# A 64-token chunk of a delta-rule recurrence on one core: three tiles of the block inverse move to the other half of the partitions, and one transpose moves behind the first level

## The reference, cut to what matters

```python
def step(S, inp):
    r_t, w_t, k_t, v_t, kk_t, a_t = inp
    sa = jnp.einsum('bhvk,bhk->bhv', S, -kk_t)
    S = (S * w_t[:, :, None, :] + sa[..., None] * (kk_t * a_t)[:, :, None, :]
         + v_t[..., None] * k_t[:, :, None, :])
    return S, jnp.einsum('bhvk,bhk->bhv', S, r_t)
```

## Time and profile before

| | us |
|---|---|
| median of 3 runs | 2737.84 |
| the three runs | 2737.84, 2742.84, 2735.46 |
| the profiled execution, its own time | 2741.77 |
| span of the profiled execution | 2740.1 |
| PE busy (share of the span) | 2511.4 (92%) |
| PE weight loads busy | 2473.5 (90%) |
| DVE busy | 1479.8 (54%) |
| ACT busy | 967.4 (35%) |
| granted clock of PE, mean | 0.935 |

### The profile page before, as it was taken

One profiled execution on the slowest core, in us unless ns is written; L12 is line 12 of the kernel. 1 busy time (PEld: TensorE's weight loads), 2 busy tenths in 40 slices (PEclk: granted clock), 3 DMA queues, 4 the chain that ended last, 5 costly groups with the idle time before them and its releaser, 6 DMA issues.

```text
span 2740.1 us, 57636 instructions
## 1 busy us (share of the span) xinstructions
PE 2511.4 (92%) x22966; PEld 2473.5 (90%) x22966; DVE 1479.8 (54%) x1889; ACT 967.4 (35%) x1159; POOL 97.5 (4%) x162
## 2 busy tenths in 40 slices
PE   8999999999999979988967546689999999999999
PEld 8999999999989978988967445589999999999999
DVE  6555555555666674544434462157565545554554
ACT  5333333333454432222202112054443333333333
POOL 0000000000110000000000000001200000000000
PEclk9999999999999989999956775589999999999999
DMA  6665665555545533333411410155555555555555
GB/s 232 209 229 184 205 218 181 182 181 184 165 164 194 174 120 123 110 101 101 134 65 33 142 67 28 52 190 188 185 183 179 182 179 182 184 180 181 182 167 174
DMA packets 120235, 432.49 MB, mean 158 GB/s; under 512 B 14232, under 2 KB 16408, under 8 KB 119328
## 3 DMA queue, kind: packets, MB, share of 16 engines
q1 hardware_dynamic: 112896, 393.49, 43.3%
q0 software_dynamic: 7200, 36.93, 3.9%
HBM read 417.34 MB, written 23.50 MB: 161 GB/s over the span
## 4 chain that ended last, share of the span: by engine, by line
PE 87%; DVE 4%; DMA 3%; DVEq 2%; ACT 2%; issue 1%; POOL 0%; ACTq 0%; SPq 0%; POOLq 0%
PE bank L249 25%; PE bank L250 25%; PE bank L251 25%; PE bank L1061 5%; DMA side<-stg 1%; PE bank L1154 1%; PE bank L1156 1%; PE bank L1163 1%; DVE qn L950 1%; PE bank L1252 1%; PE bank L1283 1%; DMA gates<-side 1%; DVE wlo L223 1%; DVE gn L915 0%; DVE nrm L812 0%
## 5 line engine op out<-in xcount | busy, mean ns | idle before, releaser
L223 DVE TENSOR_TENSOR wlo<-raw,whi 128x1024 fp32r<-128x1024 f32 (+2 forms) x762 | 907.0, 1197 | 688.5 <-ACT whi L217 680.3
L249 PE MATMUL bank<-hhi,whi 128*128 128x264 f32 x4048 | 1161.6, 287 | 24.0 <-DVE hlo L284 12.3
L250 PE MATMUL bank<-hlo,whi 128*128 128x264 f32 x4048 | 1150.7, 284 | 0.0
L251 PE MATMUL bank<-hhi,wlo 128*128 128x264 f32 x4048 | 1149.6, 284 | 0.0
L217 ACT ACTIVATE whi<-raw 128x1024 fp32r<-128x1024 f32 (+2 forms) x762 | 786.1, 1034 | 1021.9 <-PE bank L251 1017.8
L249 PEld LDWEIGHTS bank<-hhi,whi 128*128 128x128 f32 x4048 | 766.3, 189 | 31.2 <-DVE wlo L223 12.5
L250 PEld LDWEIGHTS bank<-hlo,whi 128*128 128x128 f32 x4048 | 767.1, 190 | 0.3
L251 PEld LDWEIGHTS bank<-hhi,wlo 128*128 128x128 f32 x4048 | 762.7, 188 | 0.0
L249 PE MATMUL bank<-mhi,whi 128*128 128x264 f32 x1408 | 399.6, 284 | 0.0
L250 PE MATMUL bank<-mlo,whi 128*128 128x264 f32 x1408 | 399.1, 283 | 0.0
L251 PE MATMUL bank<-mhi,wlo 128*128 128x264 f32 x1408 | 399.0, 283 | 0.0
(11 more groups left out here) (279 smaller groups left out, 1989.3 us busy)
## 6 DMA issues: line engine op xcount, KB each, us to landing
raw<-in_weights SPq DMA_DIRECT2D x666, 512.0 KB, 3.3
raw<-in_weights SPq DMA_DIRECT2D x64, 384.0 KB, 3.1
raw<-in_weights SPq DMA_DIRECT2D x32, 448.0 KB, 3.8
out_skv<-in_cache POOLq DMA_DIRECT2D x16, 512.0 KB, 3.8
side<-stg POOLq DMA_DIRECT2D x50, 132.0 KB, 3.3
gates<-side POOLq DMA_DIRECT2D x1, 4224.0 KB, 16.0
qkv<-side POOLq DMA_DIRECT2D x1, 2376.0 KB, 10.2
x<-in_x SPq DMA_DIRECT2D x4, 528.0 KB, 6.7
```

The costliest lines, as they stand in the source:

```text
L223: dve.tensor_tensor(wlo[:, s, 0:n], raw[:, s, 0:n], whi[:, s, 0:n].bitcast(F32), ALU.subtract).then_inc(lo_done, 1)
L249: pe.matmul(bank[:, 0:T], hi, xhi[:, k], start=(k == 0), stop=False)
L250: pe.matmul(bank[:, 0:T], hi, xlo[:, k], start=False, stop=False)
L251: mm = pe.matmul(bank[:, 0:T], lo, xhi[:, k], start=False, stop=(k == kt - 1))
```

## The change

`per_head` gets two arguments: `frm=1` takes the operands of head p from the other half of the partitions, and `to=1` puts the result there. `qm`, `m1` and `w1` of a head now lie in the other half. `qm` can therefore no longer be cut from `ab`. It is made from a second product `bc`·`ar` of its own (bank 3), beside `ar`·`bc` (bank 2), which is moved up from the groups behind extra(0). The wide `kc`/`ar` product takes its place behind extra(0), in banks 0 and 1. `per_head_twice` issues two groups interleaved, pair by pair: the two `ar`/`bc` products, and in levels 1 to 4 the two additions `m1`·`qm` and `qm`·`m1`. With these halves the two products of a pair and a side use all four quarters of the array. The transpose of `kc` moves behind the second groups of level 1, with a semaphore `c_kt`, and ACT's copy to `kt_` moves behind the copy of `m1` of level 1 and waits for it.

```diff
@@ -665,13 +665,16 @@
                 act.activation(pi[:], cum[:, :, cols], ACT.Exp, scale=DECAY).then_inc(c_exp, 1)
                 act.activation(vc[:], V_[:, :, cols], ACT.Copy).then_inc(c_op, 1)
                 extra(0)
-                act.wait_ge(c_pe, 9 * c + 3)
-                for dst, bank in ((vt, 1), (bt, 2), (kt_, 3)):
+                act.wait_ge(c_pe, 10 * c + 4)
+                for dst, bank in ((vt, 2), (bt, 3)):
                     act.activation(dst[:], A4[bank][:].rearrange("p (j n) -> p j n", n=C), ACT.Copy).then_inc(c_act, 1)
                 extra(1)
                 for lv in range(1, 6):
                     act.wait_ge(c_m1, 5 * c + lv)
                     act.activation(m1[:], A4[0][:].rearrange("p (j n) -> p j n", n=C), ACT.Copy).then_inc(c_act, 1)
+                    if lv == 1:
+                        act.wait_ge(c_kt, c + 1)
+                        act.activation(kt_[:], A4[3][:].rearrange("p (j n) -> p j n", n=C), ACT.Copy).then_inc(c_act, 1)
                     extra(1 + lv)
                 act.wait_ge(c_w1, 2 * c + 1)
                 act.activation(w1[:], A4[3][:].rearrange("p (j n) -> p j n", n=C), ACT.Copy).then_inc(c_act, 1)
@@ -839,25 +842,24 @@
                 dve.tensor_copy(pend[:], pc[:, :, C - 1])
                 dve.drain()
                 dve.sem_inc(c_vec, 1)
-                dve.wait_ge(c_pe, 9 * c + 1)
+                dve.wait_ge(c_pe, 10 * c + 1)
                 for q in range(2):
                     dve.tensor_tensor(ab[:, 4 * q:4 * q + 4], A4[q][:].rearrange("p (j n) -> p j n", n=2 * C),
                                       over(cc("causal"), 4), ALU.mult)
                 dve.drain()
                 dve.sem_inc(c_vec, 1)
-                dve.wait_ge(c_pe, 9 * c + 2)
-                for q in range(2):
-                    dve.tensor_tensor(ak[:, 4 * q:4 * q + 4], A4[2 + q][:].rearrange("p (j n) -> p j n", n=2 * C),
-                                      over(cc("causal"), 4), ALU.mult)
+                dve.wait_ge(c_pe, 10 * c + 2)
+                dve.tensor_tensor(tm[:], A4[2][:].rearrange("p (j n) -> p j n", n=C), over(cc("join0t"), PAIRS), ALU.mult)
+                dve.tensor_tensor(qm[:], A4[3][:].rearrange("p (j n) -> p j n", n=C), over(cc("join0"), PAIRS), ALU.mult)
                 dve.drain()
                 dve.sem_inc(c_vec, 1)
-                dve.tensor_tensor(qm[:], ab[:, :, 0:C], over(cc("join0"), PAIRS), ALU.mult)
-                extra(0)
-                dve.wait_ge(c_pe, 9 * c + 3)
-                dve.tensor_tensor(tm[:], A4[0][:].rearrange("p (j n) -> p j n", n=C), over(cc("join0t"), PAIRS), ALU.mult)
-                dve.drain()
                 dve.tensor_tensor(qm[:], qm[:], over(cc("ident64"), PAIRS), ALU.add)
                 dve.tensor_tensor(tm[:], tm[:], over(cc("ident64"), PAIRS), ALU.add)
+                extra(0)
+                dve.wait_ge(c_pe, 10 * c + 3)
+                for q in range(2):
+                    dve.tensor_tensor(ak[:, 4 * q:4 * q + 4], A4[q][:].rearrange("p (j n) -> p j n", n=2 * C),
+                                      over(cc("causal"), 4), ALU.mult)
                 for lv in range(1, 6):
                     dve.tensor_tensor(zm[:], ab[:, :, 0:C], over(cc(f"join{lv}"), PAIRS), ALU.mult)
                     dve.drain()
@@ -865,14 +867,14 @@
                     if lv == 1:
                         extra(1)
                     extra(1 + lv)
-                    dve.wait_ge(c_pe, 9 * c + 3 + lv)
+                    dve.wait_ge(c_pe, 10 * c + 4 + lv)
                     dve.tensor_tensor(qm[:], qm[:], A4[1][:].rearrange("p (j n) -> p j n", n=C), ALU.add)
                     if lv < 5:
                         dve.tensor_tensor(tm[:], tm[:], A4[2][:].rearrange("p (j n) -> p j n", n=C), ALU.add)
                 dve.drain()
                 dve.sem_inc(c_lv, 1)
                 extra(7)
-                dve.wait_ge(c_pe, 9 * c + 9)
+                dve.wait_ge(c_pe, 10 * c + 10)
                 dve.tensor_tensor(state[:], state[:], A4[2][:].rearrange("p (j n) -> p j n", n=C), ALU.add)
                 dve.tensor_copy(kkey[:, :, cols], A4[1][:].rearrange("p (j n) -> p j n", n=C))
                 dve.drain()
@@ -1053,12 +1055,25 @@
             walk(pe, name, lambda n, i: products(name, n, i, [(result(name, n), KT_OF[FIRST[name]], hi, lo)],
                                                  before if n == 0 else None))
 
-        def per_head(bank, width, col0, *terms):
+        def head(j, p, bank, width, col0, terms, frm, to):
+
+            out = bank(j)[half(p ^ to), col0(j):col0(j) + width]
+            for t, (lhs, rhs) in enumerate(terms):
+                mm = pe.matmul(out, lhs(j, p ^ frm), rhs(j, p ^ frm), start=(t == 0), stop=(t == len(terms) - 1))
+            return mm
+
+        def per_head(bank, width, col0, *terms, frm=0, to=0):
 
             for j, p in each_head():
-                out = bank(j)[half(p), col0(j):col0(j) + width]
-                for t, (lhs, rhs) in enumerate(terms):
-                    mm = pe.matmul(out, lhs(j, p), rhs(j, p), start=(t == 0), stop=(t == len(terms) - 1))
+                mm = head(j, p, bank, width, col0, terms, frm, to)
+            return mm
+
+        def per_head_twice(a, b):
+
+            for j in range(PAIRS):
+                for product in (a, b):
+                    for p in range(2):
+                        mm = head(j, p, *product)
             return mm
 
         def part(buf, lo=0, n=C):
@@ -1101,39 +1116,40 @@
                 pe.wait_ge(c_vec, 3 * c + 1)
                 pe.sem_inc(passed, 1)
                 per_head(two(0), 2 * C, lambda j: 2 * C * (j % 4), (part(bc), part(ar, 0, 2 * C))).then_inc(c_pe, 1)
-                per_head(two(2), 2 * C, lambda j: 2 * C * (j % 4), (part(kc), part(ar, 0, 2 * C))).then_inc(c_pe, 1)
+                per_head_twice((one(2), C, c64, ((part(ar), part(bc)),), 0, 0),
+                               (one(3), C, c64, ((part(bc), part(ar)),), 0, 1)).then_inc(c_pe, 1)
                 extra(0)
                 pe.wait_ge(c_op, c + 1)
                 pe.wait_ge(c_vec, 3 * c + 2)
                 pe.sem_inc(passed, 1)
-                per_head(one(0), C, c64, (part(ar), part(bc)))
-                per_head(one(1), C, c64, (part(vc), ident))
+                per_head(two(0), 2 * C, lambda j: 2 * C * (j % 4), (part(kc), part(ar, 0, 2 * C))).then_inc(c_pe, 1)
                 pe.wait_ge(c_vec, 3 * c + 3)
                 pe.sem_inc(passed, 1)
-                per_head(one(2), C, c64, (part(bc), ident))
-                per_head(one(3), C, c64, (part(kc), ident)).then_inc(c_pe, 1)
+                per_head(one(2), C, c64, (part(vc), ident))
+                per_head(one(3), C, c64, (part(bc), ident)).then_inc(c_pe, 1)
                 extra(1)
                 for lv in range(1, 6):
                     pe.wait_ge(c_lv, 6 * c + lv)
                     pe.sem_inc(passed, 1)
+                    per_head(one(0), C, c64, (part(zm), part(tm)), to=1).then_inc(c_m1, 1)
+                    extra(1 + lv, (0,))
+                    pe.wait_ge(c_act, 10 * c + (3 if lv == 1 else 3 + lv))
+                    pe.sem_inc(passed, 1)
+                    add_q = (one(1), C, c64, ((part(m1), part(qm)),), 1, 1)
+                    if lv < 5:
+                        mm = per_head_twice(add_q, (one(2), C, c64, ((part(qm), part(m1)),), 1, 0))
+                    else:
+                        mm = per_head(*add_q[:3], *add_q[3], frm=1, to=1)
+                    mm.then_inc(c_pe, 1)
                     if lv == 1:
-                        pe.wait_ge(c_act, 10 * c + 3)
-                    pe.sem_inc(passed, 1)
-                    per_head(one(0), C, c64, (part(zm), part(tm))).then_inc(c_m1, 1)
-                    extra(1 + lv, (0,))
-                    pe.wait_ge(c_act, 10 * c + 3 + lv)
-                    pe.sem_inc(passed, 1)
-                    mm = per_head(one(1), C, c64, (part(m1), part(qm)))
-                    if lv < 5:
-                        mm = per_head(one(2), C, c64, (part(qm), part(m1)))
-                    mm.then_inc(c_pe, 1)
+                        per_head(one(3), C, c64, (part(kc), ident)).then_inc(c_kt, 1)
                     extra(1 + lv, (1,))
-                per_head(one(3), C, c64, (part(ar), part(state)), (part(ak), part(vt))).then_inc(c_w1, 1)
+                per_head(one(3), C, c64, (part(ar), part(state)), (part(ak), part(vt)), to=1).then_inc(c_w1, 1)
                 extra(7, (0,))
                 pe.wait_ge(c_act, 10 * c + 9)
                 pe.wait_ge(c_lv, 6 * c + 6)
                 pe.sem_inc(passed, 1)
-                per_head(one(0), C, c64, (part(qm), part(w1))).then_inc(c_w1, 1)
+                per_head(one(0), C, c64, (part(qm), part(w1)), frm=1).then_inc(c_w1, 1)
                 extra(7, (1,))
                 pe.wait_ge(c_act, 10 * c + 10)
                 pe.sem_inc(passed, 1)
@@ -1293,6 +1309,7 @@
```

(1 more changed line is left out.)

## The result

The changed kernel takes 2749.55 us (median of 11 runs, 2743.87 to 2758.48), the kernel before 2737.84 (11 runs, 2734.01 to 2742.84). The ratio is 1.0043, with a 95% interval of 1.0029 to 1.0056: slower by 11.7 us on the medians, with an interval of 7.9 to 15.3 us. The forecast was 2746.8 us (8.9 more) in a range of 2739 to 2762. The profiled execution of the changed kernel took 2748.85 us, 7.1 more than that of before.

The account below looks back on a forecast made before the run. PE's own work was taken to bound the loop, with DVE only 0.42 us early in each level. -0.94 - 1.26 + 3.23 = +1.03 us a chunk, +4.1 for four, +4.8 for the clock: 2746.8 us, range 2739 to 2762.

Parts of the forecast that it names:

- Part 3: Level 1: ACT's splits queue behind the new kt_ wait, so PE stands idle ahead of level 2: +3.23 us a chunk.
- M: Start of level 1 on PE; the forecast counted from it, with the kt_ signal at M + 6.31.
- the later loads of SP: SP's load into the raw slot starts 4 us later, is wanted only two levels on, and costs nothing.
- The quarters: Two interleaved groups take 0.94 us; in levels 2 to 4 DVE's chain lets only 0.42 show each: -1.26 a chunk.
- (b): Rival: the quarters don't overlap by fours; +16.7 us for four chunks, 2759.3 us with the clock; chance 0.13.
- (c): Rival: starts limit the rate, two groups take 1.60 us; +11.1 us for four chunks, 2753.7 with the clock; chance 0.10.
- The start of the chunk: First stage and behind extra(0): regrouped products save 0.79 and 0.15 us, DVE's work costs nothing: -0.94 a chunk.
- The clock: After PE's mid-chunk pause the clock falls in three chunks of four, 1.6 us each: +1.2 a chunk on average.
- Rival (a): The clock holds through the pause at the start of level 2: +4.1 us, 2741.9 us; chance 0.28.
- Rival (d): ACT or DVE in level 1 is not late; only gains remain, -2.2 us a chunk, 2729 us; chance 0.05.

Follow-up runs that it names:

- e1_wait_behind: Changed kernel, with ACT's wait for the kc transpose and its copy to kt_ moved behind the two splits of level 1: 2729.20 us, ratio 0.9968.
- e5_dve_order: Kernel of e1_wait_behind, with DVE's second split and side_out moved from ahead of the two additions to behind the next zm: 2723.19 us, ratio 0.9940.
- e3_kc_only: Kernel before, with only the kc transpose moved behind level 1's second groups and ACT's kt_ copy waiting for it ahead of the splits: 2758.94 us.
- e2_sequential: Changed kernel, with per_head_twice issuing its first group whole and then its second instead of interleaved: 2756.78 us, ratio 1.0067.
- e4_fill: Changed kernel, with 24 more matmuls of unused result on PE behind level 1, where PE stands idle: 2742.10 us, ratio 1.0016.

## Why the prediction was right

**The stall.** Part 3 was +3.23 us a chunk and measured +3.25 (12.54 - 9.29). Each step is in the rows: `kt_` at M + 6.32 (forecast 6.31), the first split at M + 6.82 (6.81), DVE's second split followed, and level 2 at M + 12.54 (12.52). e1_wait_behind shows that it was this queue and nothing else. Levels 3 to 5 start with the same waits as in e1_wait_behind, so the later loads of SP cost nothing, as was said.

**The quarters.** The forecast put two interleaved groups at 0.94 us; the next group starts 0.98 after the start of the pair. The wait of 0.47 us ahead of levels 3 to 5 shows what was forecast of DVE: periods 8.91 us instead of 9.29, a gain of 0.38 against a forecast of 0.42. e5_dve_order took the wait away and got the other half. Rivals (b) and (c) fell. Of the floor of 25 ns between starts, which the Trainium skill gives in "TensorE: Matmul & The Clock Gate", section "Wait — 56ns, not 53.3ns?", the trace shows nothing between quarters: 64 starts in 0.98 us are 15 ns apart on average, for the length of a whole group.

**The start of the chunk.** From a chunk's first product to level 1 it took 21.54, 21.15, 20.96 and 20.87 us before, and 20.80, 21.32, 20.44 and 20.47 after. The slow stretches in these are 4.9 us longer after; half of that is lost time (2.5 us). Without it the starts are 1.0 us a chunk shorter, for a forecast of -0.94.

**The clock was the least certain term.** The forecast had 1.2 us a chunk, 4.8 in all. In the profiled execution the slow stretches in level 2 cost 11.60 + 10.45 + 10.45 - 3 x 8.91 = 5.8 us. The mechanism was right; that it came to three chunks of four, with one slow stretch of twice the length, was partly luck. In e3_kc_only and e2_sequential, with a pause of the same length, the clock fell in all four chunks. The length of 3.36 us from which the price was taken was the second of four in the trace of before, which go from 2.75 to 4.15 us.

The sum was 2.8 us short of the medians (8.9 against 11.7), and 8.9 lies within the interval of 7.9 to 15.3. In the loop of the profiled execution the parts are: +13.0 for level 1, -4.6 for levels 2 to 4 without the clock (forecast -5.0), -4.0 for the chunks' starts without the clock (-3.8), +5.8 for the clock in level 2 (+4.8), and +2.5 for the clock at the chunks' starts, which the forecast had not in its sum and only the other way in its range. Together that is 12.7 of the 12.8. Whether the last part belongs to the change is open: all seven other kernels have longer slow stretches there than the one profiled execution of the kernel before, by 1.5 to 7.1 us, the kernels without a stall among them.

**Rival (a)**, that the clock holds through the pause, is what e4_fill enforced: 2742.1 us, forecast 2741.9. The changed kernel itself did so in one chunk of four. Rival (d), that the splits behind the wait were not wanted, fell in the same rows as the stall was read from.

## What to carry to other kernels

When a wait is put into an engine's program, look at what is written behind it before asking how long it lasts: here a copy whose result is read only in the chunk's last products, 56 us later (1128.94 to 1185.3 in the second chunk), held back two splits that DVE, and behind DVE PE, wanted at once. Where PE is busy all the time, measure by how much the others are early before you shorten PE's work; here they were early by 0.38 us of the 0.92 saved, and reordering DVE's queue gave the rest. A pause in the middle of dense matmuls costs its own length and then perhaps the clock, so price it with and without.

## What the runs showed of the hardware

Four 64 x 64 quarters of the array work at the same time in fp32: 64 records of two groups take about the time that 32 of one take (0.98 us to the next group's start, against 0.94). Two groups issued one after the other, but in different pairs of quarters, still overlap by 0.16 us: the later group's matmuls start while some of the earlier group's have not. One and the same pause of PE, 3.2 us long, left the clock at 2.4 GHz in one chunk and let it fall to 1.2 GHz in three others, for 3.4 to 6.8 us; in two other kernels (e3_kc_only, e2_sequential) it fell in four chunks of four. With the pause filled by work that nobody uses the clock stayed at 2.4 GHz in all four. A wider spread between executions can't be laid to this. From lowest to highest it was 14.6 us for the changed kernel, 7.7 with the pause filled and 8.8 for the kernel before, but the same kernel before had 10.4 and 14.4 in two longer series.
